# Input projection of the first network with permuted columns and queries second; layer 0's weight splits behind the first job of a chunk

## The chip, the cores and the metric

The kernel runs on one core of a Trainium2 chip. The metric is the device time of one execution in microseconds (us). The kernel before takes 2006.95 us, the median of three runs (2005.91 to 2007.74).

## What is computed

Two small transformer networks run one after the other on 256 tokens of width 1024, each with two layers. Only the first one's mixer is touched here. Beside the 256 tokens `x` the first network carries 256 context tokens `cx`; both go through the same weights.

```python
IN_SIZES = (POOL_WIDTH,                              # p  256
            GLA_HEADS * GLA_DK, GLA_HEADS * GLA_DK,  # gq, gk  256, 256
            GLA_WIDTH, GLA_WIDTH,                    # gv, gg  256, 256
            GLA_GATE_RANK, GLA_GATE_RANK,            # rf, rb  16, 16
            ATTN_WIDTH, ATTN_KV_WIDTH, ATTN_KV_WIDTH)  # aq 512, ak 128, av 128

u = (rmsnorm(x, g_mix) * (1 + sc1) + sh1) @ w_in
uc = (rmsnorm(cx, g_mix) * (1 + sc1c) + sh1c) @ w_in
p, gq, gk, gv, gg, rf, rb, aq, ak, av = split_in(u)
...
la_f = jax.nn.log_sigmoid(r_f.astype(f32) @ wg[0] + bg[0]) / GLA_GATE_NORM
la_b = jax.nn.log_sigmoid(r_b.astype(f32) @ wg[1] + bg[1]) / GLA_GATE_NORM
...
mix = jnp.concatenate([pool_mixer(p, w_pool, s_pool),
                       gla_output(o_gl, gg, g_gla, x.dtype),
                       latent_attention(ql, k_all, v_all)], axis=-1) @ w_out
```

So `w_in` has 2080 columns in ten parts. Queries and keys of the attention (`aq`, `ak`) are normed per head and, for `x`, turned by rope. The gates `rf`, `rb` go through a small matrix and a log-sigmoid. In layer 1 the context is no longer updated: of its tokens only `gk`, `gv`, the gates, `ak` and `av` are needed.

## The kernel before

Each engine has a stream of its own, written out by hand in the order in which it runs; semaphores join them. Every `step` on VectorE and ScalarE waits for its own result before the next one begins.

**Precision by splitting.** Large products are made of three fp32r matmuls. A weight matrix is split into an upper part (`upper`, in `arena_r`, written by ScalarE as a rounded copy, line 1884) and the rest (`lower`, written in place in its slot of the ring, `ring_r`, by VectorE's subtraction, line 1159). `split(keys)` does one chunk, first on ScalarE, then on VectorE. There are two buffers for upper parts, so the split of a chunk waits until TensorE has finished the chunk before the current one.

**Weights.** SyncE loads all weights in the order `LOADS` into a ring of three slots of 2 MB. A slot is loaded again when TensorE has finished reading it.

**Input projection (`layer1`, from line 851 on TensorE, 1528 on VectorE, 2059 on ScalarE).** The columns are cut into five chunks, `CH1` (line 34). For each chunk and each of four token tiles of 128 (0, 1 are `x`, 2, 3 the context) there is one job of 24 matmuls (8 row blocks by three, line 535). Jobs are numbered j; they take banks of two rings in turn, `v` (VectorE copies the result into `u`, line 1542) and `a` (ScalarE does). In layer 1 (`in1_jobs`, line 145) tiles 2 and 3 leave out chunks 1 and 4, and of chunk 0 take only the 32 gate columns: 16 jobs instead of 20. Chunks before: 0 is gg and gates (288 columns), 1 is aq (512), 2 is ak, av (256), 3 is gk, gv (512), 4 is pool and gq (512).

**Order at a chunk's start.** VectorE and ScalarE first do the split of the next chunk, then the copy of the job, then `beside_in1`.

**Beside the jobs (`beside_in1`, lines 641, 1314, 1959).** When chunk 0 is through: TensorE transposes the gate columns, VectorE copies them to `rT` (line 1323). Then, one tile per job: TensorE makes z = rT x wg (two matmuls of 33 rows, into a bank of the `v` ring), VectorE takes it apart (lines 1332, 1334), ScalarE does Exp and Ln (each with its table), and VectorE subtracts (`la`, line 1159 on `GA`). `aq_sums` takes the sums of squares of the queries during chunk 2, `ak_sums` those of the keys at the first job of chunk 3 and hands the power -0.5 to GpSimd (line 2235, 128x40). `aq_norm` and `aq_rope` follow two jobs later, one tile per job, and the last of them sets `aq_ready`.

**After it (`mixer1`).** `heads` waits for `aq_ready` and transposes queries and keys; then attention steps (`attend`, with scores in the two `twin` banks), the gated part, and `fill`, which multiplies modulation weights beside it.

Of the kernel before, what the change touches and what calls it, by code (L numbers as in the profile page):

```python
# [32 lines left out]
GQ, GK, GV, GG, RF, AQ, AK, AV = 256, 512, 768, 1024, 1280, 1312, 1824, 1952  # L33
CH1 = [(1024, 1312), (1312, 1824), (1824, 2080), (512, 1024), (0, 512)]
# [156 lines left out]
def trunks(nc, a, out):  # L191
# [6 lines left out]
    with ctx:  # L198
# [314 lines left out]
        def _(pe):  # L513
# [127 lines left out]
            def beside_in1(l, j):  # L641

                if j == jobs_until(l, 1):
# [3 lines left out]
                    b, filled = take("v")  # L647
                    for t in range(4):
                        tr(b[0:32, t * P:(t + 1) * P], u[:, t, RF:RF + 32], filled if t == 3 else None)
                    mark["rT", l] = k["v"]  # L650
                t = j - jobs_until(l, 1) - 1
                if 0 <= t < 4:
                    done("v", mark["rT", l])
                    b, filled = take("v")
                    mm(b[:, :], rT[:, t * P:(t + 1) * P], par1("wg")[0:33, :], inc=filled)
                    mark["z", l, t] = k["v"]
# [109 lines left out]
            def pooling(l):  # L766
                n = S if l == L - 1 else 512
                band = par1("band").rearrange("p (t g n) -> p t g n", t=2, g=4)
                for g in range(2):
                    b, filled = take("a")  # L770
                    for s in range(n // S):
                        for par_ in range(2):
                            for t in range(2):
                                end = s == n // S - 1 and par_ == 1 and t == 1
                                mm(b[64 * par_:64 * par_ + 64, S * s:S * s + S],
                                   u[:, 2 * s + t, P * g + 64 * par_:P * g + 64 * par_ + 64],
# [361 lines left out]
        def _(dve):  # L1138
# [149 lines left out]
            def ak_sums():  # L1288

                for t in range(4):  # L1290
                    x = u[:, t, AK:AV]
# [6 lines left out]
            def aq_norm(l, t):  # L1298
                h0 = span(l, t)
                x = u[:, t, AQ + 64 * h0:AV].rearrange("p (h c) -> p h c", c=64)  # L1300
# [6 lines left out]
            def aq_rope(t):  # L1307
                table = const("rope1").rearrange("p (t c a f) -> p t c a f", t=2, c=2, a=2)
                x = u[:, t, AQ:AV].rearrange("p (h a b f) -> p h a b f", a=2, b=2, f=16)
# [4 lines left out]
            def beside_in1(l, j):  # L1314

                first, k_done = jobs_until(l, 1), jobs_until(l, 3)
                if j == first:
# [4 lines left out]
                    b = filled()  # L1322
                    step(v.tensor_copy(rT[0:32, :], b[0:32, :]), v_emptied)
                t = j - first - 3
# [3 lines left out]
                t = j - first - 1  # L1328
                if 0 <= t < 4:
                    b = filled()  # L1330
# [4 lines left out]
                                                op0=ALU.mult, op1=ALU.subtract), v_emptied)  # L1335
                t = j - (k_done - len(tiles1(l)))
                if t in tiles1(l):
                    dve.wait_ge(a_emptied, mark["job", l, jobs_until(l, 2) - 1][1])
                    aq_sums(t)
                if j == k_done:  # L1340
                    dve.wait_ge(a_emptied, mark["job", l, k_done - 1][1])
# [1028 lines left out]
```

## Time and profile before

| | |
|---|---|
| median of three runs | 2006.95 us |
| the profiled execution | 2009.39 us |
| its span | 2007.6 us |
| TensorE busy | 1788.9 us (89%) |
| VectorE busy | 1121.1 us (56%) |
| ScalarE busy | 688.0 us (34%) |
| GpSimd busy | 96.2 us (5%) |
| granted clock, mean | 0.917 |

Times in the trace count from the start of the span. PE is TensorE, PEld its weight load, DVE VectorE, ACT ScalarE, POOL GpSimd, SP SyncE (SPq its DMA queue). A matmul's duration is modelled and overlaps the next one; the time of a job is read from starts, or from the count in a stretch. PEclk is the granted clock: 1.00 is 2.4 GHz, 0.50 is 1.2 GHz.

### The profile page before, as it was taken

Reading aid. Unit: us, or ns where it says so; the run is one execution under the profiler, and the core shown is the slowest. Engines: PE = TensorE matmul, PEld = TensorE weight load, DVE = VectorE, ACT = ScalarE, POOL = GpSimd, SP = SyncE. Lnnn points to the kernel's source line nnn. Section 1 sums busy time; section 2 is a strip of 40 time slices with the busy share of each in tenths; the row PEclk is TensorE's granted clock in tenths of the full one; section 3 lists DMA queues with packets and bytes.
Section 4 is the critical chain, followed back from the end, with each engine's and each line's share of the span. In section 5 each row is a group of like instructions: output and inputs, shape, how many; then the busy total and the mean of one; then the engine's idle time right before and its main releaser. Section 6 shows DMA issues by size and latency. Waiting matters only on the chain.

```text
span 2007.6 us, 25506 instructions
## 1 busy us (share of the span) xinstructions
PE 1788.9 (89%) x10612; PEld 1454.1 (72%) x10612; DVE 1121.1 (56%) x1727; ACT 688.0 (34%) x811; POOL 96.2 (5%) x91
## 2 busy tenths in 40 slices
PE   5998888789999999988879996997899979879997
PEld 2775646677877777775558995775799756759996
DVE  3475454564445445555477675555766565566654
ACT  2323333132222122423334443454333333534331
POOL 1010001110000000010010000000100010010000
PEclk8999877899999999897889998898899989879999
DMA  8324455124333344334754545450555554325642
GB/s 325 124 86 168 169 197 202 42 75 149 133 126 126 129 159 144 105 136 147 257 192 171 203 175 206 151 190 10 161 187 164 180 199 152 126 63 182 196 159 93
DMA packets 172371, 309.20 MB, mean 154 GB/s; under 512 B 3264, under 2 KB 54720, under 8 KB 171616
## 3 DMA queue, kind: packets, MB, share of 16 engines
q1 hardware_dynamic: 168592, 293.98, 42.1%
q10 hardware_dynamic: 3376, 12.02, 1.8%
q8 instruction: 84, 1.38, 0.3%
q0 software_dynamic: 288, 1.57, 0.2%
q14 instruction: 31, 0.25, 0.0%
HBM read 305.46 MB, written 2.10 MB: 153 GB/s over the span
## 4 chain that ended last, share of the span: by engine, by line
PE 69%; DVE 16%; ACT 5%; issue 5%; DMA 3%; POOL 1%; DVEq 0%; ACTq 0%; SPq 0%; POOLq 0%
PE bank L535 53%; PE twin L535 14%; DVE ring_r L1159 4%; DVE arena L1159 3%; PE bank L544 3%; ACT arena L1884 2%; ACT arena_r L1884 2%; DMA ring<-in_w_in 2%; DMA ring<-in_w_mod 2%; POOL rs L2235 1%; DVE params L1159 1%; DVE arena_r L1159 1%; DVE X L1636 1%; DVE params L1622 0%; DVE arena L1249 0%
## 5 line engine op out<-in xcount | busy, mean ns | idle before, releaser
L535 PE MATMUL bank<-arena_r 128*128 128x512 f32 (+3 forms) x2144 | 710.2, 377 | 14.5 <-DVE arena_r L1754 6.7
L1159 DVE TENSOR_TENSOR ring_r<-ring,arena_r 128x4096 fp32r<-128x4096 f32 (+4 forms) x94 | 393.7, 4188 | 233.3 <-ACT arena_r L1884 232.7
L535 PEld LDWEIGHTS bank<-arena_r 128*128 128x128 f32 x2144 | 412.2, 192 | 95.8 <-issue 7.9
L1884 ACT ACTIVATE arena_r<-ring 128x4096 fp32r<-128x4096 f32 (+4 forms) x94 | 323.0, 3436 | 432.9 <-PE bank L535 160.5
L535 PE MATMUL twin<-actT_r,arena_r 128*128 128x256 f32 x1408 | 254.5, 284 | 1.2 <-DVE actT_r L1159 1.2
L535 PE MATMUL bank<-arena_r,actT_r 128*128 128x512 f32 (+4 forms) x640 | 227.1, 386 | 25.7 <-DVE ring_r L1159 14.2
L535 PE MATMUL bank<-ring_r,arena_r 128*128 128x512 f32 x624 | 246.0, 394 | 0.0
L1884 ACT ACTIVATE arena<-bank 128x512 f32<-128x512 f32 (+6 forms) x170 | 85.7, 504 | 426.2 <-PE bank L535 329.8
L535 PEld LDWEIGHTS twin<-actT_r,arena_r 128*128 128x128 f32 x1408 | 219.8, 192 | 2.0 <-DVE actT_r L1159 2.0
L535 PE MATMUL twin<-actT_r,ring_r 128*128 128x256 f32 x704 | 199.2, 283 | 0.0
L535 PE MATMUL bank<-ring_r,actT_r 128*128 128x512 f32 (+4 forms) x512 | 191.7, 374 | 0.0
L535 PE MATMUL bank<-actT_r,arena_r 128*128 128x512 f32 (+1 forms) x512 | 174.8, 341 | 2.8 <-issue 2.5
L535 PE MATMUL bank<-actT_r,ring_r 128*128 128x512 f32 (+1 forms) x512 | 172.1, 336 | 0.0
L535 PEld LDWEIGHTS bank<-arena_r,actT_r 128*128 128x128 f32 x640 | 127.2, 199 | 58.4 <-DVE ring_r L1159 16.6
L535 PEld LDWEIGHTS bank<-ring_r,arena_r 128*128 128x128 f32 x624 | 119.5, 191 | 25.5 <-issue 1.0
L535 PEld LDWEIGHTS twin<-actT_r,ring_r 128*128 128x128 f32 x704 | 135.2, 192 | 0.0
L2235 POOL TENSOR_TENSOR rs<-ms,neghalf 128x1 f32<-128x1 f32 (+4 forms) x44 | 45.1, 1025 | 1802.0 <-DVE ms L1173 676.7
L535 PE MATMUL bank<-ring,cpad 128*32 128x512 f32 x768 | 107.4, 685 | 23.7 <-DMA ring<-in_w_mod 22.2
L544 PE MATMUL bank<-cons,arena 128*128 128x128 f32 (+4 forms) x456 | 77.6, 327 | 50.0 <-DVE arena L1213 31.5
L535 PEld LDWEIGHTS bank<-arena 64*32 64x32 f32 (+5 forms) x1224 | 89.3, 178 | 32.9 <-DVE arena L1159 15.5
L535 PEld LDWEIGHTS bank<-ring_r,actT_r 128*128 128x128 f32 x512 | 102.4, 200 | 14.8 <-issue 1.0
L535 PE MATMUL bank<-arena 64*32 64x32 f32 (+5 forms) x1224 | 102.9, 279 | 10.9 <-DVE arena L1159 9.0
(183 smaller groups left out, 1753.0 us busy)
## 6 DMA issues: line engine op xcount, KB each, us to landing
ring<-in_w_mod SPq DMA_DIRECT2D x24, 2048.0 KB, 8.0
ring<-in_w_ada SPq DMA_DIRECT2D x24, 2048.0 KB, 8.2
ring<-in_w_gate_up SPq DMA_DIRECT2D x44, 1024.0 KB, 7.7
ring<-in_w_down SPq DMA_DIRECT2D x20, 2048.0 KB, 7.8
ring<-in_w_up SPq DMA_DIRECT2D x16, 2048.0 KB, 7.8
ring<-in_w_in SPq DMA_DIRECT2D x12, 2048.0 KB, 8.7
ring<-in_w_out SPq DMA_DIRECT2D x8, 2048.0 KB, 11.7
ring<-in_w_down SPq DMA_DIRECT2D x8, 1792.0 KB, 7.5
```

The source lines that it names most:

```text
L535: ins = nc.tensor.matmul(out_, lhsT, rhs, start=start, stop=stop)
L544: ins = nc.tensor.transpose(out_, in_, ident[0:n, 0:n])
L1159: return v.tensor_tensor(o, x, y, op)
L1636: step(v.scalar_tensor_tensor(out=X[:, t, :], in0=y2[:, t, :], scalar=rs[:, t:t + 1], in1=X[:, t, :], op0=ALU.mult, op1=ALU.add), x_ready)
L1884: return nc.scalar.activation(o, x, func, **kw)
L2235: nc.gpsimd.tensor_tensor(rs[:, at:at + n], ms[:, at:at + n], neghalf[:, at:at + n], ALU.pow)\
```

## The change

- The host orders the columns of `w_in` anew (`OLD1`), so that `u` holds GK, GV, GQ, GG, PL, AQ, AK, RF, AV. The chunks are now: 0 is ak, gates, av (288 columns), 1 is aq (512), 2 is gk, gv (512), 3 is gq, gg (512), 4 is the pool's (256).
- In layer 1, tiles 2 and 3 take chunks 0 and 2 whole and leave out 1, 3 and 4: 14 jobs.
- `rT` and z use the `twin` banks (ring `s`) instead of the `v` ring. z is made for tiles 0 and 1 at the first job after chunk 0's successor began, and for 2 and 3 two jobs later (`gate_tiles`); ScalarE does both Exp and then both Ln.
- Sums of the queries run from the second job of chunk 1 on, those of the keys at the first job of chunk 2, norm and rope from two jobs later.
- In layer 0 alone the split of the next chunk stands behind the copy of the chunk's first job and what is beside it, on VectorE and ScalarE. In layer 1 it stays in front.

```diff
-GQ, GK, GV, GG, RF, AQ, AK, AV = 256, 512, 768, 1024, 1280, 1312, 1824, 1952
-CH1 = [(1024, 1312), (1312, 1824), (1824, 2080), (512, 1024), (0, 512)]
+GK, GV, GQ, GG, PL, AQ, AK, RF, AV = 0, 256, 512, 768, 1024, 1280, 1792, 1920, 1952
+CH1 = [(1792, 2080), (1280, 1792), (0, 512), (512, 1024), (1024, 1280)]
+OLD1 = [(512, 1024), (256, 512), (1024, 1280), (0, 256), (1312, 1952), (1280, 1312), (1952, 2080)]
...
-            if l == L - 1 and t >= 2:
-                if c in (1, 4):
-                    continue
-                if c == 0:
-                    lo = RF - c0
+            if l == L - 1 and t >= 2 and c not in (0, 2):
+                continue
...
+def gate_tiles(l, j, behind):
+
+    n = j - jobs_until(l, 1) - behind
+    return [n, n + 1] if n in (0, 2) else []
...
-                    b, filled = take("v")
+                    b, filled = take("s")
                     for t in range(4):
                         tr(b[0:32, t * P:(t + 1) * P], u[:, t, RF:RF + 32], filled if t == 3 else None)
-                    mark["rT", l] = k["v"]
-                t = j - jobs_until(l, 1) - 1
-                if 0 <= t < 4:
-                    done("v", mark["rT", l])
-                    b, filled = take("v")
+                    mark["rT", l] = k["s"]
+                for t in gate_tiles(l, j, 1):
+                    done("s", mark["rT", l])
+                    b, filled = take("s")
...
-                first, k_done = jobs_until(l, 1), jobs_until(l, 3)
+                first, k_done = jobs_until(l, 1), jobs_until(l, 2)
...
-                t = j - (k_done - len(tiles1(l)))
+                t = j - jobs_until(l, 1) - 1
                 if t in tiles1(l):
-                    dve.wait_ge(a_emptied, mark["job", l, jobs_until(l, 2) - 1][1])
+                    dve.wait_ge(a_emptied, mark["job", l, j - 1][1])
                     aq_sums(t)
...
-                    if c != last_c:
-                        last_c = c
+                    if c != last_c and l > 0:
                         split(after(("in1", l, c)))
                     if r == "v":
...
                     beside_in1(l, j)
+                    if c != last_c and l == 0:
+                        split(after(("in1", l, c)))
+                    last_c = c
...
-                t = j - jobs_until(l, 1) - 2
-                if 0 <= t < 4:
-                    act.wait_ge(v_emptied, mark["z", l, t])
+                tiles = gate_tiles(l, j, 2)
+                for t in tiles:
+                    act.wait_ge(s_emptied, mark["z", l, t])
                     step(f(zt[t % 2], zt[t % 2], ACT.Exp))
+                for t in tiles:
                     step(f(zt[t % 2], zt[t % 2], ACT.Ln, bias=1.0), zlog_ready)
...
+    arrays["w_in"] = np.concatenate([x["w_in"][:, :, c0:c1] for c0, c1 in OLD1], 2)
```

## Rows read from the trace of the kernel before

**Rows 1.** The page, part 4: the chain that ended last, by engine
```profile
PE 69%; DVE 16%; ACT 5%; issue 5%; DMA 3%; POOL 1%; DVEq 0%; ACTq 0%; SPq 0%; POOLq 0%
```

**Rows 2.** Stages: window and its length, busy us (instructions) per engine, granted clock, DMA
```profile
51.78:156.40 104.62, 98.64 (x492) 82.61 (x493) 57.65 (x87) 32.84 (x31) 9.00 (x4) 0.95 0.29 101
156.40:345.00 188.60, 160.46 (x1373) 106.28 (x1371) 92.99 (x231) 63.34 (x134) 2.91 (x1) 0.78 0.56 196
...
803.60:892.00 88.40, 79.24 (x396) 65.97 (x396) 51.23 (x79) 32.43 (x31) 10.18 (x4) 0.92 0.33 111
892.00:1010.00 118.00, 103.56 (x882) 67.98 (x883) 54.38 (x135) 37.23 (x74) 1.67 (x1) 0.82 0.60 210
```

**Rows 3.** Timeline of TensorE: start, us, instruction, [idle before it and its releaser]
```profile
78.51 1.12 PE L535 MATMUL bank<-params,t 33*128 33x512 f32 x2 [0.91 <-DVE t L1323]
...
105.32 0.58 PE L535 MATMUL bank<-arena_r,actT_r 128*128 128x256 f32 x1 [5.03 <-DVE arena L1542]
...
842.49 1.47 PE L535 MATMUL bank<-params,t 33*128 33x512 f32 x2 [2.00 <-DVE arena L1542]
...
892.02 1.33 PE L544 MATMUL bank<-cons,arena 128*128 128x128 f32 x5 [5.59 <-DVE arena L1159]
```

**Rows 4.** Stretches with the granted clock, columns as in the second group
```profile
105.30:113.00 7.70, 7.68 (x49) 7.68 (x50) 7.33 (x11) 3.83 (x4) 0.00 (x0) 0.75 0.00 0
...
818.90:822.90 4.00, 4.00 (x11) 3.18 (x12) 1.14 (x1) 2.11 (x2) 0.00 (x0) 0.54 0.49 119
...
844.40:847.00 2.60, 2.60 (x14) 2.60 (x13) 1.49 (x3) 2.57 (x3) 0.00 (x0) 0.50 0.00 0
```

**Rows 5.** Stretches of one kind of job: 512, 256, 32 and 288 columns
```profile
113.00:156.40 43.40, 43.40 (x193) 35.88 (x192) 26.77 (x53) 5.81 (x5) 6.79 (x1) 1.00 0.28 97
...
850.70:853.80 3.10, 3.10 (x26) 3.10 (x26) 2.85 (x5) 0.90 (x2) 0.00 (x0) 1.00 0.00 0
...
812.20:818.90 6.70, 6.70 (x50) 6.70 (x48) 2.18 (x3) 0.41 (x1) 0.00 (x0) 0.77 0.01 2
...
54.50:66.50 12.00, 11.96 (x89) 11.68 (x88) 6.45 (x5) 3.02 (x3) 0.81 (x2) 1.00 0.22 89
```

**Rows 6.** Timelines of VectorE, ScalarE and GpSimd: steps of the projection
```profile
100.39 4.42 DVE L1159 TENSOR_TENSOR ring_r<-ring,arena_r 128x4096 fp32r<-128x4096 f32 x1 [5.76 <-ACT arena_r L1884]
...
106.03 0.69 DVE L1332 TENSOR_SCALAR GA<-bank 128x512 f32<-128x512 f32 x1
...
122.47 0.29 DVE L1159 TENSOR_TENSOR params<-arena 128x128 f32<-128x128 f32 x1
...
877.54 0.83 DVE L1159 TENSOR_TENSOR arena<-arena,rs 128x640 f32<-128x640 f32 x1 [6.35 <-POOL rs L2235]
...
883.76 0.83 DVE L1159 TENSOR_TENSOR arena<-arena,rs 128x640 f32<-128x640 f32 x1
...
96.66 3.62 ACT L1884 ACTIVATE arena_r<-ring 128x4096 fp32r<-128x4096 f32 x1
...
870.67 6.76 POOL L2235 TENSOR_TENSOR rs<-ms,neghalf 128x40 f32<-128x40 f32 x1 [63.75 <-DVE ms L1295]
```

**Rows 7.** DMA issues between 60 and 80 us: count, KB, us to landing
```profile
ring<-in_w_in SPq DMA_DIRECT2D x1, 2048.0 KB, 10.4
```

**Rows 8.** Timelines of VectorE and GpSimd where both work at once
```profile
347.98 4.41 DVE L1263 CAST actT_r<-arena 128x512 fp32r<-128x512 f32 x1
...
347.58 4.52 POOL L2257 TENSOR_TENSOR ring_r<-ring,arena_r 128x2048 fp32r<-128x2048 f32 x1 [24.66 <-ACT arena_r L1884]
...
1416.76 1.28 DVE L1636 SCALAR_TENSOR_TENSOR X<-params,rs,X 128x1024 f32<-128x1024 f32 x1
...
1416.20 0.93 POOL L2235 TENSOR_TENSOR rs<-ms,neghalf 128x1 f32<-128x1 f32 x1 [1.32 <-DVE ms L1630]
```

**Rows 9.** From the end of the projection to the first scores, both layers
```profile
156.40:169.30 12.90, 12.90 (x99) 10.87 (x97) 2.77 (x4) 5.05 (x8) 0.00 (x0) 0.87 0.47 163
892.00:906.70 14.70, 14.68 (x90) 12.40 (x90) 2.23 (x4) 4.02 (x7) 0.00 (x0) 0.69 0.41 144
```

More of the change, by code:

```diff
@@ L1321, in beside_in1 @@
                     step(v.memset(rT[32:33, :], 1.0))
-                    b = filled()
-                    step(v.tensor_copy(rT[0:32, :], b[0:32, :]), v_emptied)
-                t = j - first - 3
-                if 0 <= t < 4:
+                    b = filled("s")
+                    step(v.tensor_copy(rT[0:32, :], b[0:32, :]), s_emptied)
+                for t in gate_tiles(l, j, 3):
                     dve.wait_ge(zlog_ready, nth(zlog_ready))
                     step(tt(la[:, t, :], la[:, t, :], zt[t % 2], ALU.subtract), la_ready if t == 3 else v_step)
-                t = j - first - 1
-                if 0 <= t < 4:
-                    b = filled()
+                for t in gate_tiles(l, j, 1):
+                    b = filled("s")
                     step(v.tensor_scalar(la[:, t, :], b[:, :], 0.0, None, ALU.min))
                     step(v.scalar_tensor_tensor(out=zt[t % 2], in0=la[:, t, :], scalar=2.0, in1=b[:, :],
-                                                op0=ALU.mult, op1=ALU.subtract), v_emptied)
-                t = j - (k_done - len(tiles1(l)))
+                                                op0=ALU.mult, op1=ALU.subtract), s_emptied)
+                t = j - jobs_until(l, 1) - 1
                 if t in tiles1(l):
-                    dve.wait_ge(a_emptied, mark["job", l, jobs_until(l, 2) - 1][1])
+                    dve.wait_ge(a_emptied, mark["job", l, j - 1][1])
                     aq_sums(t)
                 if j == k_done:
-                    dve.wait_ge(a_emptied, mark["job", l, k_done - 1][1])
                     ak_sums()
-                t = j - k_done - 2
-                if 0 <= t < 4:
+                for t in range(4):
+                    if j != k_done + 2 + t:
+                        continue
                     if t == 0:
                         dve.wait_ge(rstd_ready, nth(rstd_ready))
+                    aq_norm(l, t)
                     if t < TS:
-                        aq_norm(l, t)
                         aq_rope(t)
-                    else:
-                        aq_norm(l, t)
             def heads(l):
@@ L1460, in gated_norm @@
                 dve.wait_ge(gexp_ready, nth(gexp_ready))
-                step(v.scalar_tensor_tensor(out=g, in0=g, scalar=1.0, in1=u[:, 0:n, GG:RF], op0=ALU.add, op1=ALU.mult))
+                step(v.scalar_tensor_tensor(out=g, in0=g, scalar=1.0, in1=u[:, 0:n, GG:PL], op0=ALU.add, op1=ALU.mult))
                 step(v.scalar_tensor_tensor(out=o, in0=o, scalar=0.5, in1=g, op0=ALU.mult, op1=ALU.mult), gla_ready)
@@ L2006, in gates1 @@
                 act.wait_ge(qk_ready, nth(qk_ready, n))
-                step(f(gexp[:, 0:n, :], u[:, 0:n, GG:RF], ACT.Tanh, scale=0.5), gexp_ready)
+                step(f(gexp[:, 0:n, :], u[:, 0:n, GG:PL], ACT.Tanh, scale=0.5), gexp_ready)
             def pooling(l):
@@ L2067, in layer1 @@
                 for j, (c, t, lo, hi, r) in enumerate(in1_jobs(l)):
-                    if c != last_c:
-                        last_c = c
+                    if c != last_c and l > 0:
                         split(after(("in1", l, c)))
@@ L2075, in layer1 @@
                     beside_in1(l, j)
+                    if c != last_c and l == 0:
+                        split(after(("in1", l, c)))
+                    last_c = c
+                nth(s_filled, 5)
+                nth(s_emptied, 5)
                 mixer1(l)
```

11 lines of the change are left out of this document (5 added, 6 removed).

## The prediction, made before the change was run

> **What bounds the kernel now.** I read the chain of waits first [rows 1]: TensorE holds 69% of it, VectorE 16%. So an edit pays where TensorE stands still or runs at half clock. The stages [rows 2] give the two stretches that the diff touches: the input projection of layer 0 (51.78 to 156.40 us) and of layer 1 (803.60 to 892.00). TensorE is busy 98.6 of 104.6 us and 79.2 of 88.4 us there: 15 us idle. Then the idle gaps by releaser [rows 3]: 0.91 and 5.03 us in layer 0, 2.00 and 5.59 us in layer 1, all on VectorE. Last the granted clock behind these gaps [rows 4]: it is 0.50 to 0.77 for some microseconds after each long one, so TensorE pays for a gap twice. The engines' own rows say why. The 0.91 us wait (for `rT`) and the 5.03 and 2.00 us waits (for the copy of a chunk's first job) are one pattern: VectorE's `split` of the next chunk stands ahead of that copy. The last one, 5.59 us, is `aq_ready`: norm and rope of the queries come in the last chunk.
>
> **Prices.** A 512-column job (24 matmuls) is 43.4/8 = 5.43 us [rows 5]; a 256-column one 3.0 us at full clock (26 matmuls, two of them not of the job, in 3.10) [rows 5]. A 32-column one is 6.70/2 = 3.35 us, part of it at half clock [rows 5]; a 288-column one is 12 us for 89 matmuls, or 3.2 us [rows 5]. A `split` of 4096 elements is 4.42 us on VectorE and 3.62 on ScalarE [rows 6], about half of that for 2048. Two instructions on z are 2 x 0.72 us (0.69 and the wait for the own result), one on la 0.72, the sums of one query tile 1.45 (0.69 each plus the step) [rows 6]; sums of the keys of all four tiles are eight of 0.29 and a short one, 2.8 [rows 6]. Norm and rope of one tile: 883.76 - 877.54 = 6.2 us [rows 6]. The power on GpSimd takes 6.76 us [rows 6].
>
> **Part 1, layer 0: splits behind the first job, z's in pairs on the twin banks.** The split of chunk 2 goes behind `rT`: job 4 is finished near 71.8, copy, memset and `rT` end near 73.9, and TensorE wants `rT` at 77.6. The 0.91 us go. The split of chunk 3 goes behind the copy of job 8, and z has a bank pair of its own: the 5.03 us go. With it goes the half clock behind it: two 256-column jobs took 7.7 us with a matmul of the next [rows 4] where 2 x 3.0 and that one do at full clock, 1.5 us. Sum 7.4 us. The work itself is the same: five chunks of 288, 512, 512, 512 and 256 columns, only in another order.
> What is late next? I walk VectorE and ScalarE through the new order. Chunk 2's weights are now 2 MB, asked for at 66.5 as before, when chunk 0 is read. A 2 MB load issued behind a 1 MB one landed after 10.4 us [rows 7]; alone in front it can't be later than that: 77. ScalarE's and VectorE's split then end by 85, TensorE wants them at 93. After that VectorE has z0, z1, two query sums, la, z2, z3 and so on until the key sums near 103.7; split of chunk 3 to 108 (wanted at 115); norm and rope of two tiles, two short norms; split of chunk 4 to between 127 and 134 (wanted at 136.7, since chunks 2 and 3 of 21.8 us each now stand before it). Cover is 2 us at the worst, 9 at the best. I count nothing; if the cover is gone, each microsecond costs one, and over about 2 us another 1.5 for the clock. The table loads saved on ScalarE (each pair of Exp, Ln now shares them) lie beside TensorE and count nothing. Layer 0: **-7.4 us**, bounds -7.9 (two fewer changes between projection and z) and -3.
>
> **Part 2, layer 1, what is removed.** Before: jobs 2 x 288, 2 x 32, 2 x 512, 4 x 256, 4 x 512, 2 x 512. After: 4 x 288, 2 x 512, 4 x 512, 2 x 512, 2 x 256. Two 256-column jobs go: 6.0. Two 32-column jobs become two of 288: 6.7 against 6.4, 0.3. The clock fell to half within the 32-column jobs and stayed so until 822.9: 11 matmuls in 4.0 us [rows 4] for some 2.3 at the 0.226 us of [rows 5], so 1.7. Behind the 2.00 us gap the next matmuls ran at 0.50 [rows 4] for one 256-column job and two z's: 2.4. The two waits: 2.0 and 5.6. Sum: 6.0 + 0.3 + 1.7 + 2.4 + 2.0 + 5.6 = **18.0 us**.
> The Trainium skill (TensorE: Matmul & The Clock Gate, "Wait — 56ns, not 53.3ns?") gives some 25 ns for a warm matmul of 32 columns. By that the two narrow jobs would cost 1.2 us and widening them would lose 5 us; the row has 134 ns each, so the measurement decides.
>
> **Part 3, layer 1, what comes instead.** Here splits stay first in a chunk. Start at 803.6: chunk 0 done 818.6, chunk 1 (with two z's) 832.1, z2 and z3 at 845.2, chunk 2 done 856.4, chunk 3 (two jobs) 867.3. VectorE: split of chunk 2 to 827.3, `rT` 829.3 (wanted 829.9, a cover of 0.6), z0, z1 834.0, query sum 835.5, split of chunk 3 to 840.9, job 6, query sum, key sums 845.9. Now GpSimd's power starts, and VectorE goes on to la 0, la 1, both of which read two SBUF tensors. Which of the engines gets on? [rows 8] show a VectorE cast of 512 elements taking 4.41 us while GpSimd's 4.52 us split ran, ending 0.3 us behind it; a cast of that size without it can't take longer than a copy out of PSUM, some 0.7. The other end stands there too: during the power of one element a two-input operation of VectorE took 1.28 us, with no delay seen. I take the first, since a power of 40 elements reads for longer than one of a single element; the delay is then about 6.5 us of the 6.76, else 0. With it: la 1 at 854.0, z2, z3 856.9, copy of job 8 857.6, norm and rope 863.8, la 865.3, norm and rope 871.5, and only then the split of chunk 4, to 873.9. TensorE wants it at 867.3. This is the new wait: **6.6 us**, then a half clock for two 256-column jobs, 1.5 (as in layer 0). Queries are ready near 876, chunk 4 ends at 882, so the last wait doesn't come back. Layer 1: -18.0 + 8.1 = **-9.9 us**, bounds -16 and -5.
> The Trainium skill (SBUF — State Buffer, "SBUF: two separate sides") says the port pair that VectorE and GpSimd share is held for a whole instruction. With that the sum is the one above; [rows 8] agree for the cast and not for the one-element power.
>
> **Part 4, the head of layer 1's mixer.** From 892.0 to the first scores TensorE takes 14.7 us at a clock of 0.69; layer 0 takes 12.9 at 0.87, with more transposes [rows 9]. Coming in without a gap layer 1 should gain 1.8 us; bounds 0 and 2.7. Its first three weight loads for the fills come later against the mixer's start, but the last slot is free near 882 and a load took at most 10.4 us [rows 7]; the third fill stands some 35 us in. Nothing.
>
> **Sum.** -7.4 - 9.9 - 1.8 = -19.1 us. The profiled execution took 2009.39 us around a span of 2007.6; so 1990.3 there, and from the median 2006.95: **1988 us**.
>
> **Rivals.**
> *A, VectorE isn't held up by the power.* For: the one-element row in [rows 8]. Against: the cast in the same group. Then la 1 is done at 847.3, norm and rope start when the power ends (853), and the split of chunk 4 ends near 869.6: a wait of 2.3 instead of 6.6, cold clock still likely. 4.3 us less, **1983.5**.
> *B, the cover of layer 0's last split is gone.* The queue of VectorE (norms ahead of the split of chunk 4) is 3 to 4 us later than I walked it: layer 0 loses 1 to 2 and 1.5 for the clock, layer 1's wait grows by as much, with `rT` (0.6 cover) late too. For: it is the longest queue of one engine here. Against: each step in it has its row. About **1994**.
> *C, nothing arrives.* The mixers wait for something that doesn't move with the projection, and the 19 us are given back there: **2006**. Against: every load of the weight queue waits for a slot that TensorE frees, so it moves too.
> *D, slower.* The mixers' clock. They run at 0.78 and 0.82, with 160.5 and 103.6 us of TensorE [rows 2]; their gaps move with when the clock falls. If the mean fell to 0.70 there, 264 us would become about 264 x 0.795/0.70 = 300, 36 more: 2024. It decides from a mean of 0.74 (19 us). For: the clock stands between its levels there. Against: the order of work in the mixers is the same. **2024**.
>
> **How the numbers follow.** Forecast 0.48, A 0.28, B 0.12, C 0.04, D 0.04; the rest (0.04) is a better case near 1979, bounds of parts 1 to 3 together. The range takes in forecast, A and B, with their open ends: 1979 to 1996. What a measurement of this kernel can tell from no change is about 0.2%, 4 us. Faster by more: 0.92; within: 0.04; slower: 0.04.
>
> **What would show it.** In the profile after: no gap before `rT`'s reader and before job 10 in layer 0, and a clock of 1.00 from 60 us to the end of its projection; its end near 149. In layer 1 no 32-column matmuls, clock 1.00 until near 867, then one wait of 6 to 7 us for `ring_r`, released by VectorE, with a la subtraction stretched from 0.7 to about 7 us beside the power; the end of the projection near 882. Under A that subtraction stays at 0.7 and the wait is near 2. A wait of TensorE for `twin` banks or for a load of `w_in`, or a split ahead of chunk 4 in layer 0 that is late, would make the prediction wrong; so would mixers whose length changes by more than 3 us.

## The result, and the profile after

| | before | after |
|---|---|---|
| median | 2007.33 us (2005.91 to 2007.74, 4 runs) | 1978.53 us (1975.52 to 1983.75, 4 runs) |
| ratio after / before | | 0.9861, 95% interval 0.9839 to 0.9882 |
| profiled execution | 2009.39 us | 1979.29 us |
| its span | 2007.6 us | 1977.5 us |
| granted clock, mean | 0.917 | 0.928 |

The change is 28.8 us faster between the medians. A second set of runs timed both kernels again: 1983.02 us (1978.18 to 1985.29, 6 runs) against 2006.1 (20 runs), ratio 0.989 (0.9871 to 0.9909). So the two sets put the gain at 22 to 29 us; their intervals together reach from 18 to 32. Executions of one kernel lie up to 13 us apart. Terms of a few microseconds are therefore read below from stages of a trace, and not from medians.

The chain that ended last, in the kernel after (share of the span by engine, to be read beside [rows 1]):

```profile
PE 72%; DVE 16%; ACT 5%; DMA 4%; issue 2%; POOL 1%; DVEq 0%; ACTq 0%; SPq 0%
```

The four stages of [rows 2] in the kernel after (window and its length, busy us and count of PE, PEld, DVE, ACT and POOL, then granted clock, DMA share, GB/s):

```profile
51.88:147.80 95.92, 95.82 (x493) 81.06 (x494) 57.57 (x87) 27.93 (x27) 13.08 (x4) 0.99 0.31 110
147.80:333.00 185.20, 153.07 (x1373) 102.72 (x1371) 93.07 (x231) 63.43 (x134) 2.91 (x1) 0.81 0.56 199
...
789.90:862.80 72.90, 69.01 (x348) 57.48 (x349) 51.14 (x78) 26.79 (x25) 10.63 (x4) 0.98 0.40 138
862.80:978.80 116.00, 100.80 (x879) 65.59 (x878) 53.96 (x134) 37.62 (x75) 1.67 (x1) 0.84 0.61 212
```

In layer 0 TensorE is now busy 95.82 of 95.92 us with the same number of matmuls. In layer 1 it has 48 fewer (396 to 348, two jobs of 24) and still stands 3.9 us. ScalarE's busy time falls by 5 and 6 us (four and six fewer instructions; in layer 0 they are loads of the Exp and Ln tables, 3 instead of 7 at 1.28 us), beside TensorE.

For a comparison with less in it, all traces of this case were cut at the same four events per layer: the first matmul of the projection, the first of the mixer, the first scores, and the first matmul of the output projection behind the mixer. These are lengths in us, worked out from the starts of TensorE's instructions; a wait belongs to the stage that it ends. "In" is the projection, "head" the mixer up to its first scores, "mixer" what follows. "Out, MLP" is the remainder of layer 0; "rest" goes from layer 1's output projection to TensorE's last instruction. No edit touches either:

| kernel | in, layer 0 | head | mixer | out, MLP | in, layer 1 | head | mixer | rest |
|---|---|---|---|---|---|---|---|---|
| before | 104.7 | 12.9 | 193.4 | 440.9 | 88.4 | 14.7 | 114.3 | 977.1 |
| before, again | 104.4 | 14.4 | 189.1 | 439.7 | 87.0 | 15.3 | 115.6 | 974.2 |
| after | 95.9 | 13.6 | 189.1 | 439.5 | 72.9 | 13.7 | 114.3 | 977.3 |
| after, again | 95.9 | 13.0 | 192.4 | 439.2 | 73.0 | 12.2 | 117.7 | 975.0 |

The two stages that the diff rewrites repeat within 0.3 us, except layer 1 before (88.4 and 87.0). They give -8.8 and -15.5 us (-14.1 against the second trace of before). The untouched stages don't repeat: layer 0's mixer takes 189 or 193 us under either kernel. Of the 30.1 us between the first two spans, 4.3 are that mixer, on its faster side by chance. Without it the change is worth some 26 us.

TensorE's one long wait that is left in the two projections, and its first matmuls in the mixer, where [rows 3] had 5.59 us:

```profile
855.48 0.39 PE L539 MATMUL bank<-arena_r,actT_r 128*128 128x256 f32 x1 [2.27 <-DVE ring_r L1162]
...
862.81 0.82 PE L548 MATMUL bank<-cons,arena 128*128 128x128 f32 x6
```

The 5.03, 2.00 and 5.59 us of [rows 3] are gone, and so is the 0.91 before z. In their place stands one wait, of the predicted kind (TensorE for the `split` of the last chunk in layer 1) and a third of the predicted size: 2.27 for 6.6 us. VectorE's side of it:

```profile
831.81 0.69 DVE L1162 TENSOR_TENSOR GA<-GA,t 128x512 f32<-128x512 f32 x1
832.53 0.69 DVE L1162 TENSOR_TENSOR GA<-GA,zspare 128x512 f32<-128x512 f32 x1
...
846.90 0.83 DVE L1162 TENSOR_TENSOR arena<-arena,rs 128x640 f32<-128x640 f32 x1
...
853.14 2.29 DVE L1162 TENSOR_TENSOR ring_r<-ring,arena_r 128x2048 fp32r<-128x2048 f32 x1
```

And GpSimd's powers, in layer 0 and in layer 1:

```profile
103.47 10.89 POOL L2241 TENSOR_TENSOR rs<-ms,neghalf 128x40 f32<-128x40 f32 x1 [48.08 <-DVE ms L1298]
...
831.98 7.14 POOL L2241 TENSOR_TENSOR rs<-ms,neghalf 128x40 f32<-128x40 f32 x1 [38.76 <-DVE ms L1298]
```

The second power runs from 831.98 to 839.12. The first la subtraction of VectorE began 0.17 us before it, the second lies wholly beside it; both take 0.69 us, the duration that they have anywhere else. The prediction had one of them stretched to about 7 us. It is the power that is longer, by 0.4 us in layer 1 and by 4.1 in layer 0.

### The profile page after: what moved, and what is told of

It is laid out like the page before. It is cut to its first block, busy times and chain, and to the rows that moved or that the text cites. A ratio compares the mean times of both kernels' runs of the same rounds, so it can differ in the third digit from the quotient of the medians.

```text
span 1977.5 us, 25394 instructions
## 1 busy us (share of the span) xinstructions
PE 1761.8 (89%) x10564; PEld 1435.1 (73%) x10564; DVE 1121.2 (57%) x1726; ACT 677.6 (34%) x802; POOL 101.2 (5%) x91
## 4 chain that ended last, share of the span: by engine, by line
PE 72%; DVE 16%; ACT 5%; DMA 4%; issue 2%; POOL 1%; DVEq 0%; ACTq 0%; SPq 0%
PE bank L539 55%; PE twin L539 14%; DVE ring_r L1162 4%; DVE arena L1162 3%; PE bank L548 3%; ACT arena_r L1885 2%; ACT arena L1885 2%; DMA ring<-in_w_in 2%; DMA ring<-in_w_mod 2%; DVE arena_r L1162 1%; POOL rs L2241 1%; DVE params L1162 1%; DVE arena L1252 1%; DVE X L1637 1%; DVE params L1623 0%
## 5 line engine op out<-in xcount | busy, mean ns | idle before, releaser
L539 PE MATMUL bank<-arena_r 128*128 128x512 f32 (+2 forms) x2128 | 705.9, 378 | 16.1 <-DVE arena_r L1755 6.7
L539 PE MATMUL bank<-arena_r,actT_r 128*128 128x512 f32 (+3 forms) x624 | 219.1, 382 | 25.4 <-DVE ring_r L1162 18.3
L1885 ACT ACTIVATE arena<-bank 128x512 f32<-128x512 f32 (+5 forms) x169 | 85.5, 506 | 406.9 <-PE bank L539 311.2
L539 PE MATMUL bank<-ring_r,actT_r 128*128 128x512 f32 (+3 forms) x496 | 184.6, 372 | 0.0
L539 PEld LDWEIGHTS bank<-arena_r,actT_r 128*128 128x128 f32 x624 | 120.8, 194 | 54.5 <-DVE ring_r L1162 21.1
L2241 POOL TENSOR_TENSOR rs<-ms,neghalf 128x1 f32<-128x1 f32 (+4 forms) x44 | 49.6, 1126 | 1762.0 <-DVE ms L1176 680.7
L539 PE MATMUL bank<-ring,cpad 128*32 128x512 f32 x768 | 103.2, 662 | 23.8 <-DMA ring<-in_w_mod 22.3
L548 PE MATMUL bank<-cons,arena 128*128 128x128 f32 (+3 forms) x448 | 74.0, 319 | 45.4 <-DVE arena L1216 32.9
L539 PEld LDWEIGHTS bank<-actT_r,arena_r 128*128 128x128 f32 x512 | 97.9, 191 | 16.1 <-issue 5.6
## 6 DMA issues: line engine op xcount, KB each, us to landing
ring<-in_w_out SPq DMA_DIRECT2D x8, 2048.0 KB, 12.2
```

The lines of the kernel that those rows point to most:

```text
L539: ins = nc.tensor.matmul(out_, lhsT, rhs, start=start, stop=stop)
L548: ins = nc.tensor.transpose(out_, in_, ident[0:n, 0:n])
L1885: return nc.scalar.activation(o, x, func, **kw)
L2241: nc.gpsimd.tensor_tensor(rs[:, at:at + n], ms[:, at:at + n], neghalf[:, at:at + n], ALU.pow)\
```

## The experiments

There are nine runs: seven kernels with parts of the change or one thing added, and both kernels once more. VectorE's subtraction (splits, la, norms) is line 1159 in kernels made from `before` and 1162 in those made from `after`.

### The order alone

From `before`: on VectorE and ScalarE, in layer 0, the split goes behind the first copy and what is beside it. Columns and banks stay.

```diff
-                    if c != last_c:
-                        last_c = c
+                    if c != last_c and l > 0:
                         split(after(("in1", l, c)))
...
                     beside_in1(l, j)
+                    if c != last_c and l == 0:
+                        split(after(("in1", l, c)))
+                    last_c = c
```

> The kernel before with one part of the change: in layer 0 the split of the next chunk stands behind the copy of the chunk's first job and what is beside it, on VectorE and ScalarE. Columns, jobs and the banks of z are as before. Theory (the two waits of layer 0 come from the place of the split alone): the waits of 0.9 and 5.0 us and the half clock behind the second (1.5 us) go, the stage of layer 0 falls from 104.6 to about 97 us, layer 1's stage stays at 88.4; total 7 to 8 us less, 0.9962 of before. Rival (the v ring, which z shares with the jobs, is what holds TensorE, so the order without z on banks of its own brings only the 0.9): 103 us for the stage, total 0.9995.

Measured: median 2000.41 us (9 runs), ratio 0.9968 (0.9954 to 0.9981). Layer 0's stage is 101.3 us long, 3.4 less than before; layer 1's is 88.4, unchanged. Both halves of the split of chunk 3 and TensorE's wait for it:

```profile
99.54 3.62 ACT L1886 ACTIVATE arena_r<-ring 128x4096 fp32r<-128x4096 f32 x1
...
103.27 4.43 DVE L1159 TENSOR_TENSOR ring_r<-ring,arena_r 128x4096 fp32r<-128x4096 f32 x1 [3.96 <-ACT arena_r L1886]
...
107.75 0.50 PE L535 MATMUL bank<-arena_r,actT_r 128*128 128x512 f32 x1 [2.71 <-DVE ring_r L1159]
```

With the old columns the chunk before it is only 256 wide. Four of its jobs don't last long enough to cover a split that begins behind the first of them: it ends at 107.70, and TensorE starts at 107.75. VectorE's half is late because it waits 3.96 us for ScalarE's. That one runs at 99.54, where [rows 6] had it at 96.66: in ScalarE's queue, too, the split has moved back, behind another tile's Exp and Ln, which take 1.9 us each with their table loads. The waits of 0.91 and 5.03 us are gone, one of 2.71 is new, with a clock of 0.66 for the 5 us behind it. Moved alone, the split brings less than half of what the whole change brings in layer 0.

### The columns and banks alone

From `after`: in layer 0 the splits stand in front again, as everywhere before.

```diff
-                    if c != last_c and l > 0:
+                    if c != last_c:
                         split(after(("in1", l, c)))
...
-                    if c != last_c and l == 0:
-                        split(after(("in1", l, c)))
                     last_c = c
```

> The changed kernel without its order of splits: in layer 0 too the split of the next chunk comes first, on both engines; columns, jobs, norms and the banks of z are the changed ones. Theory (order and columns lean on each other: chunk 2 now brings 2 MB, which land near 74.5 us and are split on VectorE by 82.8, and rT stands behind that split): TensorE waits near 77.4 for rT until about 84.7, 7 us, then at half clock for some microseconds; the stage of layer 0 is 95.9 + 7.3 + 1.5 or more, 104 to 107 us; layer 1's stage stays at 72.9; total 9 to 11 us above the changed kernel. Rival (the columns alone bring the gain of layer 0, the order is incidental): stage near 96 to 98, total within 2 us of the changed kernel.

Measured: median 1992.82 us (4 runs), ratio 0.993 (0.9916 to 0.9945). Layer 0's stage takes 106.6 us, 1.9 more than before the change; layer 1's takes 72.9, exactly as in `after`. TensorE in layer 0:

```profile
85.16 1.22 PE L539 MATMUL twin<-params,t 33*128 33x512 f32 x1 [7.47 <-DVE t L1326]
```

Chunk 2 is 512 wide now, so its split is twice as long, and z stands behind `rT`, and `rT` behind that split. So layer 0's 8.8 us need the order, and layer 1's 15.5 don't.

### The z's on the old bank ring

From `after`: `rT` and z take banks of the `v` ring again, that VectorE's copies of the jobs also use.

```diff
-                    b, filled = take("s")
+                    b, filled = take("v")
...
-                for t in gate_tiles(l, j, 1):
-                    done("s", mark["rT", l])
-                    b, filled = take("s")
+                for t in gate_tiles(l, j, 1):
+                    done("v", mark["rT", l])
+                    b, filled = take("v")
```

> The changed kernel with rT and z back in the v ring, in pairs as in the changed kernel. Theory (the twin banks are what lets z wait for VectorE without holding the jobs): job 6 needs the bank of z0, which VectorE empties only behind the split of chunk 2 (near 84.4 us in layer 0), so TensorE waits about 4.5 us there in layer 0 and about 1.5 in layer 1, with a half clock behind the first; total 6 to 9 us more than the changed kernel. Rival (VectorE is in time anyway, the banks are free of effect): within 1 us.

Measured: median 1994.68 us (7 runs), ratio 0.995 (0.9929 to 0.997). The stages are 103.5 and 78.6 us, so 7.6 and 5.7 longer than in `after`, together 13.3; 6 to 9 had been expected, with only 1.5 of it in layer 1. The longest gaps of TensorE, one in each layer:

```profile
85.89 0.80 PE L539 MATMUL bank<-arena_r,actT_r 128*128 128x512 f32 x1 [4.64 <-DVE t L1335]
...
852.42 0.79 PE L539 MATMUL bank<-arena_r,actT_r 128*128 128x512 f32 x1 [3.49 <-DVE t L1335]
```

The jobs now wait for a bank that VectorE empties of z behind its other work (line 1335 is the last instruction that reads z). There is a second gap of 0.8 us of this kind in either layer, and one of 0.76 for the last split in layer 1. The rest of the 13.3 us lies at half clock behind the long gaps (0.50 from 83.5 to 90.2 and from 851.5 to 858.2). The change's least visible edit, the ring, carries over 13 us of it. The prediction had put the 5.03 us of [rows 3] down to both, the order and the banks; these three runs agree: order alone -3.4, columns and banks without the order +1.9, order and columns without the banks 103.5 - 104.7 = -1.2, all three -8.8.

### No narrow jobs

From `before`: tiles 2 and 3 compute all of chunk 0 in layer 1, 288 columns instead of 32. Nobody reads the others.

```diff
-                if c == 0:
-                    lo = RF - c0
```

> The kernel before, but in layer 1 the jobs of tiles 2 and 3 in chunk 0 take all 288 columns instead of the 32 of the gates (the extra columns are never read). Theory (narrow jobs cost as much as wide ones and bring the clock down): no stretch at half clock behind chunk 0, the stage of layer 1 falls from 88.4 to about 86.4 us; total 2 us less. Rival (a narrow job is cheap, its price in the trace is an artefact of the records): the stage grows by 2 x 3.2 less what the narrow ones really took, total 2 to 5 us more. Rival 2 (the clock falls there anyhow): stage unchanged within 0.5 us.

Measured: median 2005.65 us (10 runs), ratio 0.9988 (0.9974 to 1.0002). Layer 1's stage is 84.0 us long against 88.4 and 87.0 in the two traces of `before`. The stretch of the two jobs, then the one that answers to the 4.00 us in [rows 4], and the one around the later gap:

```profile
810.00:816.30 6.30, 6.30 (x50) 6.30 (x49) 2.54 (x3) 0.41 (x1) 0.00 (x0) 1.00 0.01 3
816.30:820.30 4.00, 4.00 (x20) 3.31 (x19) 1.22 (x1) 2.33 (x2) 0.00 (x0) 1.00 0.56 154
...
838.10:842.60 4.50, 4.20 (x27) 3.27 (x27) 3.37 (x5) 3.06 (x3) 0.00 (x0) 1.00 0.01 4
```

And the two narrow jobs of `before`, one after the other:

```profile
812.10:814.70 2.60, 2.60 (x26) 2.60 (x25) 2.08 (x2) 0.41 (x1) 0.00 (x0) 1.00 0.02 6
814.70:818.80 4.10, 4.10 (x26) 4.10 (x26) 0.19 (x1) 0.00 (x0) 0.00 (x0) 0.63 0.00 0
```

So the 3.35 us of the prediction are the mean of two different jobs: at full clock a 32-column job takes 2.60 us, and a 288-column one takes 3.16, start to start. More columns take less time here only because of the clock. It fell to 0.50 in the second narrow job in each of the three traces that have narrow jobs (both of `before` and the order alone), and at this place in none of the eight that don't. From the first of the two jobs to the end of the two 512-column jobs behind them it is 21.1 us in each of the three and 18.85 here: widening brings 2.3 us, where the prediction had 0.3 + 1.7.

The other 2.2 us of the 4.5 come later, behind the 2.00 us gap. It is still there, and in this execution the clock held behind it. From it to the end of the last job TensorE took 41.3 us, where `before` took 43.9 and 42.5; 0.5 of that is given back in the wait for `aq_ready`, now 6.06 us. In the two traces of `before` it fell, but not for equally long:

```profile
843.10:849.90 6.80, 6.80 (x27) 5.69 (x26) 3.18 (x5) 5.95 (x7) 0.00 (x0) 0.50 0.01 2
```

```profile
840.70:844.00 3.30, 3.19 (x14) 2.79 (x14) 2.52 (x4) 2.74 (x3) 0.00 (x0) 0.50 0.02 5
844.10:849.90 5.80, 5.80 (x41) 4.87 (x40) 3.99 (x7) 4.91 (x7) 0.00 (x0) 1.00 0.00 0
```

That is the whole of the 1.4 us between 88.4 and 87.0. Whether the wide jobs had a part in the clock holding behind the gap, one trace can't tell. The totals differ by 2.4 us, with an interval from 5.2 us faster to 0.4 slower, so this gain is seen in the stage alone.

### Who holds up whom: GpSimd's power and VectorE

From `after`: three short instructions of VectorE (a memset of `sqk`) stand between the sums that the power waits for and the next instruction with two inputs. So the power surely starts first.

```diff
                 handed.append(("power", 0, 40))
+                step(v.memset(sqk, 0.0))
+                step(v.memset(sqk, 0.0))
+                step(v.memset(sqk, 0.0))
```

> The changed kernel with three memsets of 128x128 (no SBUF input) on VectorE right behind the instruction that hands the power to GpSimd, in both layers; so the power starts first, and VectorE's split of 4096 elements (layer 0) and the la subtractions (layer 1), each with two SBUF inputs, start while it is under way. Theory A (the power takes its inputs at its start and holds up nobody after that): split 4.42 us, subtractions 0.69, power 6.8 us in both layers; total as the changed kernel within 1 us. Theory B, that of the prediction (the power holds VectorE's two-input instructions up until it ends, and only VectorE's head start hid that in the changed kernel): split about 10.5 us, the first subtraction about 7; TensorE's wait ahead of layer 1's last chunk grows from 2.3 to about 8 us; total 6 us more. Theory C (VectorE always goes first): power stretched to 10.5 us or more in layer 0, split 4.42.

Measured: median 1980.54 us (4 runs), ratio 0.9862 (0.984 to 0.9883). GpSimd and VectorE in layer 0, then in layer 1:

```profile
105.83 6.79 POOL L2244 TENSOR_TENSOR rs<-ms,neghalf 128x40 f32<-128x40 f32 x1 [48.02 <-DVE ms L1298]
106.42 4.43 DVE L1162 TENSOR_TENSOR ring_r<-ring,arena_r 128x4096 fp32r<-128x4096 f32 x1
...
839.57 6.76 POOL L2244 TENSOR_TENSOR rs<-ms,neghalf 128x40 f32<-128x40 f32 x1 [40.30 <-DVE ms L1298]
840.18 0.69 DVE L1162 TENSOR_TENSOR GA<-GA,t 128x512 f32<-128x512 f32 x1
```

This is what tells the theories apart. The power starts at 105.83 and runs 6.79 us, as long as it runs alone. VectorE's split of two SBUF inputs begins 0.59 us later, wholly inside it, and takes 4.43 us, as long as it takes alone. The la subtraction beside the other power keeps its 0.69. So a power that began 0.6 us earlier holds nobody, and it isn't stretched by what begins later either. In `after` it is the other way round: the split began at 103.29, the power 0.18 us behind it, and the power took 10.89 us, 4.1 more than alone, about the length of the split.

The kernel with the columns and banks alone is a control for that. In its layer 0 a la subtraction of 0.68 us stood 0.18 us ahead of the power, and not the split:

```profile
117.10 7.16 POOL L2237 TENSOR_TENSOR rs<-ms,neghalf 128x40 f32<-128x40 f32 x1 [61.70 <-DVE ms L1298]
```

The power is 0.4 us longer and not 4.1, as in layer 1 of `after`. In all eleven traces it takes 10.89 us behind a split, 7.14 to 7.16 behind a la subtraction, and 6.76 to 6.79 where no instruction with two SBUF inputs has just begun. The one-element power in [rows 8] fits. With 0.93 us it is longer than the 0.55 of most of its kind, and in the trace before an instruction of VectorE with two inputs had begun 0.16 us ahead of it:

```profile
1416.04 0.68 DVE L1159 TENSOR_TENSOR params<-params,GA 128x512 f32<-128x512 f32 x1
```

The Trainium skill (SBUF — State Buffer, "SBUF: two separate sides") says that of the two engines whichever starts first gets the shared pair for its whole instruction and the other fully blocks. The 10.89 us agree with that, with VectorE first. The 4.43 and 0.69 us with the power first don't, and the measurement decides.

### The norms two jobs later

From `after`: norm and rope of the two tiles come two jobs later, so the split of the last chunk is no longer behind them.

```diff
-                    if j != k_done + 2 + t:
+                    if j != k_done + 4 + t:
```

> The changed kernel with norm and rope of queries and keys two jobs later (from the fourth job behind the key sums instead of the second). Their sums, the power, columns, splits and banks stay. Theory (taking the queries second is worth the wait for aq_ready at the end of layer 1's stage, 5.6 us before, because norm and rope then end ahead of TensorE; the wait of 2.3 us for the last split is the price of it in VectorE's queue): in layer 1 norm and rope of two tiles now begin at the third chunk's end, about 854 in the changed kernel's time, the last split stands ahead of them and its 2.3 us go, but aq_ready comes near 869 where TensorE asks for it near 861: a wait of 7 to 9 us, stage of layer 1 78 to 80 us instead of 72.9; layer 0's stage 95.9 as in the changed kernel or up to 2 more; total 5 to 8 us above the changed kernel. Rival (the order of the norms is free of effect, the gain of layer 1 is that of the jobs left out): stage of layer 1 within 1.5 us of 72.9.

Measured: median 1986.02 us (4 runs), ratio 0.9905 (0.9881 to 0.9929). The stage takes 74.5 us, 1.6 more than in `after`. TensorE's first wait in the mixer, and the start of the norms on VectorE:

```profile
867.94 0.90 PE L548 MATMUL bank<-cons,arena 128*128 128x128 f32 x3 [3.89 <-DVE arena L1162]
...
853.70 0.82 DVE L1162 TENSOR_TENSOR arena<-arena,rs 128x640 f32<-128x640 f32 x1
```

The wait for the split is gone and the one for `aq_ready` is back, 3.89 us, as [rows 3] had it with 5.59. The stage is longer by less than was expected, 1.6 us (3.89 - 2.27) and not 5 to 7: TensorE asked for the queries at 864.05, later than assumed, so less of the norms lay open. That is also hardly outside the 1.5 us that the rival, norms without effect, allowed. What speaks against the rival is the wait's new place and releaser, not the length. Only the place of the wait is shown by this run, not a gain or loss of the whole: its median is 3.0 us above the nearest one of `after`, less than executions differ.

### The split between the two norms

From `after`: in layer 1 VectorE's split of the last chunk stands between norm and rope of the first tile and that of the second.

```diff
-                    if c != last_c and l > 0:
+                    if c != last_c and l > 0 and c != 3:
                         split(after(("in1", l, c)))
...
+                    if l > 0 and t == 1:
+                        split([("in1", l, 4)])
                     aq_norm(l, t)
```

> The changed kernel, and in layer 1 VectorE splits the last chunk ahead of the second tile's norm and rope instead of behind it (ScalarE's part stays). Theory (the one wait left in layer 1's stage, 2.3 us for this split, is set by the queue of VectorE, and the half clock behind it and into the mixer's head hangs on the wait): the wait goes, the clock stays at 1.00 to the end of the stage, layer 1's stage falls from 72.9 to between 69 and 70 us and the head of the mixer by up to 1; queries are ready at the same time, near 857.5 in the changed kernel's time, 1.5 us before TensorE comes to them. Total 4 to 5 us less than the changed kernel, 0.984 of before. Rival (the wait passes to aq_ready, or is absorbed in the mixer): total within 1.5 us of the changed kernel.

Measured: median 1975.18 us (1969.12 to 1979.04, 5 runs), ratio 0.9852 (0.9829 to 0.9874). The stage and the mixer's head:

```profile
790.00:858.80 68.80, 67.20 (x349) 56.01 (x350) 51.04 (x78) 26.71 (x25) 10.63 (x4) 1.00 0.40 136
858.80:871.50 12.70, 12.06 (x90) 10.12 (x88) 2.23 (x4) 4.41 (x8) 0.00 (x0) 0.87 0.59 214
```

Neither wait is there: the queries are ready before TensorE asks, and so is the split. The stage is 4.0 us shorter than in `after`, with the clock at 1.00. Of these, 2.3 us are the wait. The rest is the clock, which fell once in this stage in both traces of `after`, once behind the wait and once far ahead of it; that it held here is one execution and may be chance. The median is 7.8 us under that of `after` in the same set of runs; 4 to 5 of these are seen in the trace, the rest is of the size by which executions differ. This has the lowest median of the kernels here. That it beats `after` rests on the wait that is gone; the ratios to `before`, 0.9852 and 0.989, have intervals that just overlap.

### The two kernels again

> The kernel before itself, for the same purpose. Theory: projection stages 104.6 and 88.4 within 0.3 us, or layer 1's shorter by up to 2.4 where the clock happens to hold over its 2.0 us wait; first mixer from 189 to 195. Rival: first mixer 193.4 again within 1 us.

> The changed kernel itself, for the length of each stage in a second execution and for the spread of its times. Theory (the first mixer's length, 189.1 us in its first profile against 193.4 before, is not the change's: it moves from execution to execution with the phases of the clock): the two projection stages repeat within 0.3 us (95.9 and 72.9), the first mixer comes out anywhere from 189 to 195. Rival (the mixer is shorter because the projection ends otherwise): 189 again within 1 us.

Measured: 2008.28 us (2003.68 to 2011.89, 12 runs; 1.0015 of its neighbours, 1.0001 to 1.003) and 1983.02 us. Their stages stand in the table at the start, and came out as expected: the projections repeat, except that layer 1's of `before` is 1.4 us shorter, and layer 0's mixer moves under either kernel. The clock behind the new wait of `after` in its first trace, then in its second:

```profile
856.70:860.00 3.30, 3.30 (x17) 3.30 (x17) 0.69 (x3) 0.00 (x0) 0.00 (x0) 0.50 0.89 286
```

```profile
797.50:800.80 3.30, 3.30 (x16) 3.30 (x15) 2.68 (x1) 0.52 (x1) 0.00 (x0) 0.50 0.21 77
...
859.50:862.00 2.50, 2.47 (x20) 2.47 (x21) 1.86 (x5) 0.00 (x0) 0.00 (x0) 1.00 0.34 64
```

The same gap of 2.27 us costs the clock in one execution (17 matmuls in 3.30 us) and not in the other (20 in 2.50). There the clock fell at the start of the stage instead, behind a wait of 1.29 us that both have, and the stage came out equally long.

## Why the prediction was right, and where it wasn't

**The time.** Faster by over 0.2% came true. The forecast was 1988 in a range from 1979 to 1996, and rival A 1983.5. The medians are 1978.53 and 1983.02: the first lies 0.5 us under the range, the second in it, on A. The forecast's own mechanism, the power's hold, didn't occur; A's did. The first median is under A's number by terms that are named below, and the untouched mixer of layer 0 was 4.3 us short in its profiled execution. The change brought a fifth to a half more than the 19.1 us of the forecast. That its median still meets the range, or nearly, is owed to the range's low end, which stood for a better case of parts 1 to 3 and for A, and not to the forecast's own sum.

**Part 1, layer 0: -7.4 predicted, -8.8 measured.** Right in its places: no wait ahead of z, none at the old job 10, clock 0.99, end at 147.80 for "near 149". The splits behind the first job were all in time, so rival B fell. The term for a 256-column job was too large; four of them stand here in a stretch of their own:

```profile
136.40:147.80 11.40, 11.40 (x98) 11.40 (x97) 0.85 (x2) 0.98 (x2) 0.00 (x0) 1.00 0.52 185
```

That is 2.85 us and not 3.0. By this the half clock of [rows 4] cost 7.7 - 2 x 2.85 - 0.23 = 1.8, not 1.5. With the two waits that makes 7.7. The last 1.1 has no row of its own. The two fewer changes between projection and z, for which the prediction had allowed 0.5, are the only thing known to go there.

**Part 2, what layer 1 loses.** Two jobs went, 48 matmuls, now 5.7 us instead of 6.0. The narrow jobs and their clock were right in sum, 0.3 + 1.7 predicted and 2.3 us in the run that only widened them; the split between the two wasn't, since 3.35 us was no price of a narrow job but the mean of 2.60 at full clock and 4.1 mostly at half. For the clock behind the 2.00 us gap 2.4 had been put down; against that run, where it held, it cost 2.7 us in one trace of `before` and 1.3 in the other. The waits of 2.0 and 5.6 went. The Trainium skill (TensorE: Matmul & The Clock Gate, "Wait — 56ns, not 53.3ns?") has some 25 ns for a warm matmul of 32 columns, by which widening should have lost 5 us. The 26 matmuls in 2.60 us show 100 ns and more at full clock. So widening alone would have lost 1.1 us (2 x 0.56), and with the clock it gained 2.3.

**Part 3, the new wait: the step that failed.** Its place, its kind and its releaser were right, its size wasn't: 6.6 us predicted, 2.27 measured. The step that failed is "I take the first", the choice of the cast in [rows 8] as the nearest row for what a power does to VectorE. It was chosen because a power of 40 elements would read for longer than one of a single element. The runs show no delay: 0.69 us beside the power in `after`, 4.43 and 0.69 with the power started first. The other row of the same group, the 1.28 us step with no delay beside the one-element power, was the one to follow, since it had the same instruction on GpSimd. The cast's partner was another operation, one that streams 2048 elements; the power reads two times 40 elements and is busy for 6.8 us. How long GpSimd is busy doesn't tell the two apart, since 4.52 us held and 6.8 us didn't. That a power reads its 80 elements at its start and needs nothing shared after that is the likely reason and isn't shown: in the cast's row VectorE's instruction was another one, too. That a power under way holds up no two-input instruction is shown. With 2.3 for 6.6 the prediction's own walk would have had layer 1 at -14.2, which is the -14.1 and near the -15.5 measured. The half clock behind the wait, put at 1.5, came in one of two traces (17 matmuls in 3.30 us, some 1.3 more than at the 0.12 us each of full clock); in the other as much came at the stage's start.

**What remains in layer 1.** Between -14.2 and -15.5 are 1.3 us. As much lies between the two traces of `before` (88.4 and 87.0), whose waits are the same and whose clock stood at 0.50 for 6.8 and for 3.4 us behind the 2.00 us gap.

**Part 4, the mixer's head: -1.8 predicted.** 14.7 and 15.3 us became 13.7 and 12.2; the means differ by 2.0. Layer 0's head, where nothing changed, moves by as much as 1.5 between executions, so this agrees with the forecast and doesn't prove it. Its stretch in the first trace of `after`, which answers to the second line of [rows 9]:

```profile
862.80:876.50 13.70, 13.08 (x90) 10.59 (x88) 2.23 (x4) 4.41 (x8) 0.00 (x0) 0.77 0.45 157
```

The clock rose from 0.69 to 0.77, the way the argument had it.

**Rivals C and D.** Nothing was given back: layer 1's mixer is 114.3 us in both first traces, layer 0's 189 to 193 in both kernels. The sign by which the prediction wanted to judge this, "mixers whose length changes by more than 3 us", did appear by its letter, 193.4 against 189.1 in the first traces. But it was too narrow: the same kernel's own executions differ by 3.3 there (189.1 and 192.4 in `after`) and by 4.3 (193.4 and 189.1 in `before`). It couldn't have convicted anything. The mixers' clock was 0.81 and 0.84 against 0.78 and 0.82, so rival D had it the wrong way round.

**The sum.** Predicted -19.1, and -23.4 with A's wait. The stages give -8.8, -14.1 to -15.5, and -2.0: about -25.6. The difference is the 1.4 of layer 0 and the scatter of layer 1.

## What to carry to other kernels

When a long instruction of GpSimd runs beside VectorE, don't price the contention by how long it is busy; see which of the two starts first, and look for a row with the same instruction, even a much smaller one, before one of the same length. Where work is reordered so that it hides behind a job, check that job's length in the new and the old cut, and the ring of banks that both share: the three edits here give -3.4, +1.9 and -8.8 us in layer 0 depending on which of them are together. And once a wait is gone, walk the slowest queue once more: one step moved between two others took the last wait, 2.3 us. Before a mean becomes the price of a job, look at the clock within it: 3.35 us were 2.60 and 4.1.

## What the runs showed of the hardware that was not expected

- A power of 128x40 on GpSimd takes 6.76 to 6.79 us alone and doesn't slow a VectorE instruction with two SBUF inputs that begins 0.6 us into it (4.43 and 0.69 us beside it, 4.42 and 0.69 without). A split of VectorE that begins 0.18 us before it stretches it to 10.89 us, a subtraction of 0.69 us to 7.14.
- A job of 24 matmuls, each with a 128x128 weight load, takes 2.60 us with 32 columns at full clock, 2.85 with 256, 3.16 with 288 and 5.43 with 512. A ninth of the columns saves less than a fifth of the time. The clock fell to 0.50 in the second of two 32-column jobs in three traces of three, and the pair then took longer than two of 288 columns (6.75 against 6.32 us).
- The same gap of about 2 us in the same place lowered the granted clock in one execution and not, or not for as long, in another: to 0.50 for 6.8 us, for 3.4 us and not at all behind the 2.00 us gap (two traces of `before` and the one with wide jobs), for 3.4 us and not at all behind the 2.27 us gap. The price of the clock behind such a gap is a range from nothing to 2.7 us in these stages.
- Executions of one kernel lie 2 to 13 us apart, and one untouched stage takes either 189 or some 193 us. A term below that is read in its own stage.
